# A diffusion backbone layer: the last two expert down projections in column halves, a split scatter, one gating product on GpSimd

## The reference

```python
h = _rmsnorm(x, g_norm1) * (1 + scale1) + shift1
proj = h @ w_in + b_in
x = x + gate1 * (merged @ w_out)          # merged: mLSTM branch and pooling branch
h2 = _rmsnorm(x, g_norm2) * (1 + scale2) + shift2
x = x + gate2 * _hier_moe(h2, ...)
y = _rmsnorm(x, g_final)
```

## Time and profile before

| What | Value |
|---|---|
| Median of 3 runs | 946.25 us (945.71 to 946.47) |
| The profiled execution's own time | 948.32 us |
| Its span in the profile | 946.3 us |
| TensorE busy, share of the span | 924.8 us, 98% |
| VectorE busy | 746.2 us, 79% |
| ScalarE busy | 498.0 us, 53% |
| GpSimd busy | 78.8 us, 8% |
| Mean granted TensorE clock | 0.993 |
| Chain that ended last | PE 92%, DVE 4%, DMA 2%, ACT 1% |

### The profile page before, as it was taken

The page is one execution under the profiler, slowest core; times in us unless marked ns, Lnnn a source line. Parts: engine busy times, 40 slices in busy tenths (PEclk is TensorE's granted clock), DMA queues, the critical chain, the costliest instruction groups (busy, mean ns, idle before and its releaser), DMA issues.

```text
span 946.3 us, 14234 instructions
## 1 busy us (share of the span) xinstructions
PE 924.8 (98%) x5550; PEld 815.4 (86%) x5550; DVE 746.2 (79%) x1038; ACT 498.0 (53%) x660; POOL 78.8 (8%) x91
## 2 busy tenths in 40 slices
PE   7999999999999999999999999989999999999996
PEld 5799999899888999999999998868888888888872
DVE  5798889897494478889464465489999999999998
ACT  5464343343133356576312232257887887887873
POOL 0010110100001010101000000011112111111110
PEclk9999999999999999999999999999999999999998
DMA  9916675574656242434392136179999999999965
GB/s 367 357 60 193 216 231 204 177 266 157 223 198 210 82 127 76 139 124 149 135 358 77 62 125 275 68 257 411 397 422 421 420 407 422 418 410 414 397 265 201
DMA packets 41458, 234.63 MB, mean 248 GB/s; under 512 B 4560, under 2 KB 5008, under 8 KB 20912
## 3 DMA queue, kind: packets, MB, share of 16 engines
q1 hardware_dynamic: 26928, 180.12, 49.5%
q0 software_dynamic: 10720, 44.32, 13.2%
q10 hardware_dynamic: 3744, 9.28, 2.6%
HBM read 208.43 MB, written 25.28 MB: 247 GB/s over the span
## 4 chain that ended last, share of the span: by engine, by line
PE 92%; DVE 4%; DMA 2%; ACT 1%; issue 1%; SPq 0%; DVEq 0%; POOLq 0%; ACTq 0%
PE ps L2067 86%; PE ps L2127 2%; PE ps L2588 1%; DMA raw<-in_wst 1%; PE ps L2630 1%; PE ps L2114 1%; DMA xg<-h2scr,slot_rows 0%; PE ps L2314 0%; PE ps L2425 0%; DVE rowA L2022 0%; DVE xr L2025 0%; DVE xr L2031 0%; PE ps L2502 0%; DVE RP L1359 0%; ACT ghi L774 0%
## 5 line engine op out<-in xcount | busy, mean ns | idle before, releaser
L1848 DVE TENSOR_TENSOR wlo<-raw,whi 128x2048 fp32r<-128x2048 f32 x32 | 72.5, 2289 | 4.2 <-ACT whi L1066 4.0
L1848 DVE TENSOR_TENSOR olo<-raw,ohi 128x2048 fp32r<-128x2048 f32 x32 | 72.4, 2287 | 3.9 <-ACT ohi L1066 3.9
L2067 PE MATMUL ps<-Thi,ghi 128*128 128x320 f32 x224 | 71.1, 317 | 0.0
L1066 ACT ACTIVATE whi<-raw 128x2048 fp32r<-128x2048 f32 x32 | 61.3, 1918 | 18.4 <-PE ps L2067 18.4
L1066 ACT ACTIVATE ohi<-raw 128x2048 fp32r<-128x2048 f32 x32 | 61.3, 1917 | 18.0 <-PE ps L2067 18.0
L2067 PE MATMUL ps<-Tlo,ghi 128*128 128x320 f32 x224 | 69.5, 310 | 0.0
L707 ACT ACTIVATE whi<-raw 128x2048 fp32r<-128x2048 f32 x14 | 26.8, 1912 | 69.7 <-PE ps L2067 69.7
L2067 PEld LDWEIGHTS ps<-Thi,ghi 128*128 128x128 f32 x224 | 42.3, 189 | 11.7 <-issue 10.9
L2067 PE MATMUL ps<-hhi,ghi 128*128 128x320 f32 x168 | 52.3, 311 | 0.0
L2067 PE MATMUL ps<-hlo,ghi 128*128 128x320 f32 x168 | 52.2, 311 | 0.0
L2067 PE MATMUL ps<-hhi,whi 128*128 128x320 f32 x224 | 51.4, 310 | 0.0
(11 more groups left out here) (450 smaller groups left out, 2653.8 us busy)
## 6 DMA issues: line engine op xcount, KB each, us to landing
raw<-in_wexp SPq DMA_DIRECT2D x64, 1024.0 KB, 8.5
raw<-in_wst SPq DMA_DIRECT2D x59, 1024.0 KB, 6.0
eraw<-in_wexp SPq DMA_DIRECT2D x32, 1024.0 KB, 9.1
thscr<-gout ACTq DMA_DIRECT2D x20, 320.0 KB, 5.2
nm<-negscr POOLq DMA_DIRECT2D x8, 640.0 KB, 6.8
wib<-wiscr POOLq DMA_DIRECT2D x8, 512.0 KB, 5.9
TH<-thscr POOLq DMA_DIRECT2D x3, 1280.0 KB, 6.3
xT<-in_x SPq DMA_DIRECT2D x4, 640.0 KB, 5.8
```

The source lines that it names most:

```text
L1066: act.activation(ehi[i % ESPL][:, :], eraw[s][:, :], ACT.Copy).then_inc(e_hi, 1)
L1848: dve.tensor_tensor(elo[i % ESPL][:, :], eraw[s][:, :], f32(ehi[i % ESPL][:, :]), ALU.subtract).then_inc(e_free[s], 1)
L2067: return nc.tensor.matmul(out, lhsT, rhs, start=start, stop=stop)
```

## The change

Experts 14 and 15 (the last two of the list) no longer make both banks side by side. `down_halves` first makes all 12 matmuls of columns 0 to 511, then the 12 of columns 512 to 1023; the transposes of expert 15's inner product stay in the middle of expert 14's. ScalarE copies each half out by itself (`rows_half`). For expert 14, GpSimd scatters each half on its own, through a view of `yscr` with 2562 half rows whose indices (`half_rows`) VectorE computes once, at expert 1. The last tile's product of `rowA` and `gate2` moves from VectorE to GpSimd, and VectorE and the last of SyncE's five `rowB` loads wait for it (`g_sent`). The first `scale_rows` on ScalarE moves ahead of the last `expert_hi`, and with it the wait for `d_ga`. TensorE begins its final part with the first halves of tiles 0 and 1.

```diff
--- before.py
+++ after.py
@@ -377,6 +377,7 @@
         rank = at("rank", 205.875, [P, 2, NT])
         wab = at("wab", 205.9375, [P, 2, NT])
         thr = at("thr", 206, [P, 8])
+        half_rows = at("half_rows", 6.9375, [P, 2], I32)
         slot_rows = at("slot_rows", 206.0625, [P, 2, NE], I32)
 
         modscr = nc.dram_tensor("modscr", (64, P), F32, kind="Internal").ap()
@@ -434,13 +435,14 @@
             "s_lg", "s_am_ex", "s_cnt", "s_oh", "s_rk_tab", "s_idx", "s_round", "s_wab"))
         e_full = [sem(f"e_full{s}") for s in range(ERAW)]
         e_free = [sem(f"e_free{s}") for s in range(ERAW)]
-        e_hi, e_lo, e_mm, e_th, e_act, e_part, e_aTp, e_aTh, e_aTl, e_xT, e_xgh, e_xgl, e_y = (
-            sem(n) for n in ("e_hi", "e_lo", "e_mm", "e_th", "e_act", "e_part", "e_aTp", "e_aTh",
+        e_hi, d_half, e_mm, e_th, e_act, e_part, e_aTp, e_aTh, e_aTl, e_xT, e_xgh, e_xgl, e_y = (
+            sem(n) for n in ("e_hi", "d_half", "e_mm", "e_th", "e_act", "e_part", "e_aTp", "e_aTh",
                              "e_aTl", "e_xT", "e_xgh", "e_xgl", "e_y"))
         f_a, f_b, f_c, f_y, f_sq, f_rs, f_out, s_out, s_sum1 = (sem(n) for n in (
             "f_a", "f_b", "f_c", "f_y", "f_sq", "f_rs", "f_out", "s_out", "s_sum1"))
         s_sto, p_go, v_go, y_sent = (sem(n) for n in ("s_sto", "pool_go", "dve_go", "y_sent"))
         g_sent, f_ps, s_lt = sem("g_sent"), sem("f_ps"), sem("s_lt")
+        e_down_half = sem("e_down_half")
         a_steps, v_steps, g_steps = sem("act_steps"), sem("dve_steps"), sem("pool_steps")
         v_item = sem("dve_item_steps")
 
@@ -544,8 +546,11 @@
                             broadcast_row(gate2[:, v, :], 3, v).then_inc(d_tail, 16)
                 sp.wait_ge(d_tail, (r + 2) * 48 - 48)
                 sp.dma_start(gfin[:, :], gf_d.partition_broadcast(P)).then_inc(d_tail, 16)
+                sp.wait_ge(d_half, r * 16 + 16)
                 sp.wait_ge(d_sc, r * (16 * NE) + 16 * (NE - 1))
                 for t in range(NT):
+                    if t == NT - 1:
+                        sp.wait_ge(g_sent, 2 * r + 3)
                     sp.dma_start(rowB[:, t, :], yscr[1 + T + t * P:1 + T + (t + 1) * P, :])\
                       .then_inc(d_gb[t], 16)
                 sp.wait_ge(s_cnt, 1)
@@ -657,19 +662,32 @@
             def scatter(r, p):
                 if p:
                     gp.wait_ge(d_sc, r * (16 * NE) + 16 * p)
+                    if p == NE - 1:
+                        gp.wait_ge(d_half, r * 16 + 16)
                     gp.sem_inc(y_sent, 1)
                 if p == NE - 1:
                     for t in range(NT):
                         gp.wait_ge(d_gb[t], (r + 2) * 16)
-                gp.wait_ge(e_y, r * NE + p + 2)
+                gp.wait_ge(e_y, r * (NE + 2) + (p + 2 if p < NE - 1 else NE + 3))
                 gp.sem_inc(p_go, 1)
                 e = expert_at(p)
-                gp.indirect_dma_start(yscr, bass.IndirectOffsetOnAxis(
-                    ap=slot_rows[:, 1, e:e + 1], axis=0), yb[p % 2][:, :], None).then_inc(d_sc, 16)
-                if p == NE - 2:
+                if p != NE - 2:
+                    gp.indirect_dma_start(yscr, bass.IndirectOffsetOnAxis(
+                        ap=slot_rows[:, 1, e:e + 1], axis=0), yb[p % 2][:, :], None).then_inc(d_sc, 16)
+                else:
+                    for a, done in ((0, d_half), (1, d_sc)):
+                        if a:
+                            gp.wait_ge(e_y, r * (NE + 2) + NE + 1)
+                            gp.sem_inc(p_go, 1)
+                        gp.indirect_dma_start(yscr.rearrange("r (a n) -> (r a) n", a=2),
+                                              bass.IndirectOffsetOnAxis(ap=half_rows[:, a:a + 1], axis=0),
+                                              yb[p % 2][:, a * 512:(a + 1) * 512], None).then_inc(done, 16)
                     gp.wait_ge(g_sent, 2 * r + 2)
                     gp.sem_inc(p_go, 1)
-                    gp.memset(tick[:, :], 0.0).then_inc(g_sent, 1)
+                    gp.wait_ge(d_tail, r * 48 + 48)
+                    gp.wait_ge(f_a, (r + 2) * NT)
+                    gp.tensor_tensor(rowA[:, NT - 1, :], rowA[:, NT - 1, :], gate2[:, 1, :], ALU.mult)\
+                      .then_inc(g_sent, 1)
 
             gp.memset(tick[:, :], 0.0).then_inc(g_sent, 1)
             with gp.Fori(0, last_round) as r:
@@ -1087,6 +1105,15 @@
                                    ps[:, DOWN_BANK[p]:DOWN_BANK[p] + 2, :],
                                    ACT.Copy).then_inc(e_y, 1)
 
+                def rows_half(p, a):
+                    y, n = yb[p % 2], slice(a * 512, (a + 1) * 512)
+                    if a == 0:
+                        act.wait_ge(y_sent, r * NE + p + 1)
+                        act.wait_ge(e_down_half, 2 * r + p - NE + 3)
+                    else:
+                        act.wait_ge(e_mm, r * RCH + down_at(p) + 2 + ESPL)
+                    act.activation(y[:, n], ps[:, DOWN_BANK[p] + a, :], ACT.Copy).then_inc(e_y, 1)
+
                 def scale_rows(ts):
                     for t in ts:
                         act.activation(rowA[:, t, :], rowA[:, t, :], ACT.Copy,
@@ -1112,6 +1139,10 @@
                     else:
                         tokens_hi(1)
                     expert_hi(c + 2)
+                    if p == NE - 1:
+                        act.wait_ge(s_wab, r + 1)
+                        act.wait_ge(d_ga, r * 16 + 16)
+                        scale_rows(range(1))
                     expert_hi(c + 3)
                     if 0 < p < NE - 1:
                         tokens_hi(p + 1)
@@ -1125,12 +1156,13 @@
                 act.activation(oh_T[:, 0:4, :], ps[:, 6, :].rearrange("p (t n) -> p t n", n=P), ACT.Copy)
                 act.activation(oh_T[:, 4, :], ps[:, 7, 0:P], ACT.Copy)
                 inner_hi(NE - 1)
-                act.wait_ge(s_wab, r + 1)
-                act.wait_ge(d_ga, r * 16 + 16)
-                scale_rows(range(2))
-                rows_out(NE - 2)
-                scale_rows(range(2, NT))
-                rows_out(NE - 1)
+                rows_half(NE - 2, 0)
+                scale_rows(range(1, 2))
+                rows_half(NE - 2, 1)
+                scale_rows(range(2, 4))
+                rows_half(NE - 1, 0)
+                scale_rows(range(4, NT))
+                rows_half(NE - 1, 1)
                 act.wait_ge(s_cnt, 1)
                 act.reg_load(last_round, rounds_i[0:1, 0:1])
 
@@ -1973,6 +2005,9 @@
                         choice(1)
                     if p == 1:
                         dve.wait_ge(s_rk_tab, 2 * r + 3)
+                        e = NE + expert_at(NE - 2)
+                        for a in range(2):
+                            dve.tensor_scalar(half_rows[:, a:a + 1], ps[:, 5, e:e + 1], 2.0, float(a), ALU.mult, ALU.add)
                         dve.tensor_copy(slots[:, :, 1:EE], found[1][:, :, 1:EE]).then_inc(s_idx, 1)
                         count_rounds()
                     expert_lo(c + 1)
@@ -2012,7 +2047,7 @@
                    .then_inc(f_b, 1)
 
             def base_add(t):
-                dve.wait_ge(f_b, t + 1)
+                dve.wait_ge(f_b, min(t + 1, NT - 1))
                 dve.tensor_tensor(xr[:, t, :], xr[:, t, :], rowA[:, t, :], ALU.add).then_inc(f_c, 1)
 
             def combine(t):
@@ -2032,9 +2067,11 @@
                                          ALU.mult, ALU.mult).then_inc(f_out, 1)
 
             base(0)
-            for t in range(1, NT):
+            for t in range(1, NT - 1):
                 base(t)
                 base_add(t - 1)
+            base_add(NT - 2)
+            dve.wait_ge(g_sent, 2 * rounds + 1)
             base_add(NT - 1)
             dve.wait_ge(f_c, NT)
             combine(0)
@@ -2631,10 +2668,9 @@
                                                    act_[:, f * P:(f + 1) * P], ident)
                     last.then_inc(e_aTp, 1)
 
-                def down(p, between=None):
+                def down(p):
                     pe.wait_ge(e_aTl, r * NE + p + 1)
-                    if p < NE - 1:
-                        pe.wait_ge(e_y, r * NE + p + 1)
+                    pe.wait_ge(e_y, r * (NE + 2) + p + 1)
                     for c in range(2):
                         hi, lo = chunk(down_at(p) + c)
                         for f2 in range(2):
@@ -2645,10 +2681,28 @@
                             last = three(groups, aTh[p][:, f, :], aTl[p][:, f, :], hi, lo,
                                          f == 0, f == FT - 1)
                         last.then_inc(e_mm, 1)
-                        if between is not None and c == 0:
-                            between(p + 1)
-
-                pe.wait_ge(e_y, r * NE + 1)
+
+                def down_halves(p, between=None):
+                    pe.wait_ge(e_aTl, r * NE + p + 1)
+                    if p < NE - 1:
+                        pe.wait_ge(e_y, r * (NE + 2) + p + 1)
+                    w = [chunk(down_at(p)), chunk(down_at(p) + 1)]
```

(25 more changed lines are left out.)

## The result

| | before | after |
|---|---|---|
| median, us (lowest to highest, runs) | 946.88 (945.71 to 948.44, 8) | 950.01 (948.97 to 950.75, 8) |
| ratio, 95% interval | | 1.003 [1.0021, 1.0039] |
| profiled execution: own time / span | 948.32 / 946.3 | 950.22 / 948.3 |
| granted clock, mean | 0.993 | 0.994 |

The change makes the kernel slower by 2.85 us (2.0 to 3.7 by the interval; the medians alone differ by 3.13). The prediction of 946.5 us, no change, was wrong. Timed twice more among the experiments, with one small edit that is described there, the change gave 1.0014 [1.0005, 1.0023] and 1.0019 [1.001, 1.0028], 1.3 and 1.8 us. It is slower each time, and the three intervals share only a narrow stretch at 1.0021 to 1.0023.

A forecast was written before the change was run, and what follows sets the result against it. VectorE was taken to set the start of `combine(0)`, 0.3 us late, while on TensorE -1.1 us (stop removed) and +1.1 to +1.4 us (stop added) cancel. From 946.25 us it forecast 946.5, no tellable change; range 945.2 to 948.1.

The forecast's parts named there:

- VectorE's loss beside it: VectorE's base operations beside GpSimd's product: time lost there, bounded by 0 and 3.0 us, taken as 0.5 us.
- the nearest row: VectorE's operation at 914.25 beside GpSimd's DMA issue at 914.89: still 1.22 us, so read as a loss of 0.
- second rival: VectorE and GpSimd delay each other, 919.7 to 924: 947.0 to 948.1 for a 1 to 2 us loss; chance 0.20.
- deciding point: Second rival decides if VectorE loses over 1 us at 919.7 to 924, or the product takes over 3.4 us.
- Stop before `last_rows` gone, -1.1: TensorE between expert 15's down projection and `last_rows`: the 1.11 us stop for the row copy-out goes, -1.1 us.
- New stop of 1.1 to 1.4 ahead of expert 15, by `d_ga`: TensorE before expert 15's down projection: the late `rowA` load delays ScalarE, VectorE and then TensorE, +1.1 to +1.4 us.
- first rival: ScalarE before chunk 95: `rowA` lands by 906.4, no `d_ga` stop, 0.4 to 1.1 us gained, 945.2 to 945.9; chance 0.12.
- Scatter 0 to 0.6 us sooner, took 0.3: Expert 14's half scatter leaves 256 KB rather than 512 KB to write; `rowB` 0 to 0.6 us sooner, taken as 0.3.
- third rival: Expert 14's second half scatter is issued late, `rowB` lands 0.6 to 1.1 us later, 946.8 to 947.4; chance 0.07.
- Product from 919.7, 3.0 us long: GpSimd's product of tile 4: starts at 919.7, ends at 922.7, just before VectorE wants it at 923.0.
- Margin of 1.0 us on VectorE: VectorE's slack before `combine(0)`: 1.0 us, used up by the base operations' later start.
- What would show it wrong: No TensorE stop before expert 15's projection, base operations much over 1.22 us, or `combine(0)` over 1 us from 924.7.

The follow-up runs named there:

- e10: e3 with expert 14's rows scattered whole, after both halves are copied out; 947.90 us, 1.0004 against the kernel before.
- e2: The changed kernel with tile 0's scale and its `d_ga` wait back behind `aTh_last`, product still on GpSimd; 948.27 us, 1.0006 against before.
- e3: The changed kernel with product back on VectorE and tile 0's scale back in place, only the column halves kept; 947.03 us, 0.9995 against before.
- e9: e3 with the first `rowB` tile loaded in two column halves; 947.34 us, 1.0005 against the kernel before.
- e4: The kernel before with the product on GpSimd as its only change; 947.28 us, 1.0004 against before.
- two controls: The changed kernel with VectorE rereading the number of rounds at expert 8, timed twice; 948.37 and 949.14 us, 1.0014 and 1.0019 against before.

## Why the prediction was wrong

**The step that failed is one term: "VectorE's loss beside it", taken as 0.5 us, measured 2.15 us.** I bounded it by 0 and 3.0 us and took a value near the lower end by "the nearest row", VectorE's 1.22 us beside GpSimd's DMA issue. That row shows the wrong direction. Between an issue and VectorE it is the issue that gives way (0.96 to 1.96 us for expert 14's rows in these runs, VectorE's operation beside it always 1.21 to 1.23), and before's 1.42 us for the issue was itself a sign of it. And an issue isn't a product that reads two SBUF operands. The number 1.22 was right, but not near what I used it for. The Trainium skill says in GPSIMD Engine Reference, "Key points", that there is contention, which I cited; its page SBUF — State Buffer ("Who interferes with whom" and "SBUF: two separate sides") says more, and I hadn't weighed it: a VectorE instruction with two SBUF inputs and a GpSimd instruction that reads SBUF take turns for whole instructions, and the second blocks. For the products the traces agree (2.15, 2.15, 1.07 us).

Put 2.15 in place of 0.5 and the prediction's own line gives 913.9 + 9 x 1.135 + 0.08 + 2.15 = 926.3, against the 926.0 measured. It is the second rival, "VectorE and GpSimd hold each other up", which I gave 0.20, with its deciding point (a loss over 1 us) and its place right. The range ended at a loss of 2 us, 948.1, just short of it: by the same sum a loss of 2.15 is 946.25 + 1.95 = 948.2. The measured 950.01 lies another 1.8 us above. Of that, 0.6 us is the kernel before itself, whose eight runs have a median of 946.88 where three had 946.25; the other 1.2 us no term of the prediction covers, and it is taken up under what stays open.

The other steps, in their order:
- *Stop before `last_rows` gone, -1.1*: right (919.03 to 919.26, no stop).
- *New stop of 1.1 to 1.4 ahead of expert 15, by `d_ga`*: right in place and cause. On the load side it is 1.20 us, on the matmul side 0.77, less than forecast. ScalarE's idle stretch ended at 907.7, forecast 908.0; the series began at 913.55, forecast 913.9. The first rival, no stop, was wrong.
- *Scatter 0 to 0.6 us sooner, took 0.3*: 0.53 by e10. In after it only had to make `rowB` not late.
- *The halves don't bring the scatter forward*, third rival: not in after, whose issues took 0.96 us each. In e2, e3 and e9 the second took 1.95 to 1.96.
- *Product from 919.7, 3.0 us long*: 918.46 and 3.05. The start was 1.2 us off: ScalarE's scaling of tile 4 began at 917.24 and not 917.8, and GpSimd followed its end by 0.07 us and not 0.8. The size was right for a wrong reason. It isn't three streams in a row, but 0.85 us of waiting for VectorE and 2.2 us of work (below).
- *Margin of 1.0 us on VectorE*: right, and decisive. e4 shows that it alone would have swallowed the offload's loss.
- *What would show it wrong*: I had named base operations much longer than 1.22 us, and `combine(0)` more than 1 us from 924.7. Both came (3.37; 926.04).

The offload saves VectorE 1.135 us and takes 2.15 from it, a net loss of 1.0 us on VectorE. It shows in the time only where VectorE has no margin left, as e4 and after show.

**What stays open.** The traces of after and its two controls put the cost at 1.5 to 1.8 us at `combine(0)`, the timings at 2.85, 1.3 and 1.8. The profiled execution of after adds some 0.4 us in its last store. The rest of the first timing's excess, 0.9 us by the ratio, isn't explained. Nor do the runs show what the column halves are worth by themselves: e3 is level with before, but with the stretched second issue.

## What to carry to other kernels

Before moving an elementwise operation from VectorE to GpSimd to relieve VectorE, check what VectorE does meanwhile: beside two-input SBUF operations a product of this size cost it 2.15 us to save 1.14. Price a resource that no row shows from the end of the range with the nearest *kind of access*, not from whichever row is nearest in time. And read a moved wait with its transfer: of the two faults here, one is mended by loading 9.5 us sooner, with no instruction of ScalarE, VectorE or TensorE moved.
